# A DeltaNet solve with 16x16 blocks on VectorE, joined to 32x32 on TensorE

## The chip, the cores and the metric

The kernel runs on one core of a Trainium2 chip. The metric is the device time of one execution in microseconds (us); lower is better. Below, TensorE is PE (its weight loads PEld), VectorE DVE, ScalarE ACT, GpSimd POOL and SyncE SP.

## What is computed

A two-layer decoder trunk over 256 tokens of width 2048, float32: layer 0 mixes with mLSTM and retention heads, layer 1 with a gated DeltaNet, each followed by a SwiGLU FFN. The change lies in the DeltaNet of layer 1. It has 32 value heads and works in chunks; for each head it solves a unit lower triangular system with the strictly lower matrix `a`:

```python
k_beta = k * beta[..., None]
a = jnp.where(strict, jnp.einsum('bhnld,bhnsd->bhnls', k_beta, k) * decay, 0.0)
rhs = jnp.concatenate([v * beta[..., None], k_beta * jnp.exp(g_cum)[..., None]], axis=-1)
sol = lax.linalg.triangular_solve(a, rhs, left_side=True, lower=True, unit_diagonal=True)
```

The kernel computes the inverse T of (I + a) explicitly, in chunks of 128 tokens: first the inverses of small diagonal blocks, then larger ones from pairs. With blocks T1 above, T2 below and A21 between, the lower left block of the joined inverse is -T2 A21 T1.

## The kernel before

All big matrix products stream their weights in *units*: 512 KB of weights (two tiles of 128 rows by 512 columns) are loaded by SP into one of four buffers `wraw`; ACT rounds them to `whi` (L957), DVE makes the remainder `wlo` (L1386), and PE multiplies: eight products with `whi` (L527, L528), then four with `wlo` (L533). A unit's buffers are free again when PE has finished it, so ACT and DVE may run at most four units ahead; PE waits for `whi` at the start of a unit and for `wlo` before the four low products. The input projection of layer 1 has 192 units.

The DeltaNet itself is woven into these units in four *rounds* of 8 heads x 2 chunks (16 systems each), which start at units 20, 57, 94 and 131 and have 43 *slots*. After each unit every engine calls `gdn(r, s)` with the slot's number. PE does slot s behind unit start + s; ACT and DVE do it behind their piece of unit start + s + 2 (`AHEAD`), so slot s of DVE stands two units ahead of PE's in the order of the weights. Each engine runs its own instructions strictly in this order. Below, "unit n" is the nth after a round's start and Pn is the start of its four low products.

What a round does around the change:

- slots 7 and 8: DVE builds the systems `A_` (L1764); slot 9: DVE convolves V0 (L1747, 12 instructions), ACT gathers the 32x32 diagonal blocks into `diag` (L1243); POOL clears `TT` and `T`.
- slot 10: DVE turns the diagonal blocks within quarters of 32 partitions (`leaf_start`: a transpose of 1024 elements a partition, L1771, and a copy of 512, L1773). Each partition then works on one system's block: 16 systems, the even columns in one half of a quarter's 32 partitions and the odd ones in the other.
- slots 10 to 20: `leaf` does 31 elimination steps, three a slot; each is a product (L1782) and a subtraction (L1785) with a drain behind each. The inverse's transposes `leaf_T` and `leaf_TT` are made in slot 20 (`leaf_end`, L1789 and L1792).
- slot 13: PE turns V0 (L732), and ACT copies it (L1210); slot 15: PE turns Q (L580), and ACT takes its taps from PSUM (L1181), each behind its `whi`.
- slot 21: ACT copies `leaf_TT` into `TT` (L1259), POOL copies `leaf_T` into `T` (L496); DVE convolves Q.
- slots 23, 24: PE joins 32x32 inverses to 64x64, first `level_q` (L772), then, after a copy by ACT, `level_t` (L780, L782); slots 27, 28: 64x64 to 128x128 (L765).
- In the last round DVE has, besides, products of gates with outputs (L1889) at units 146 and 149, which are slots 13 and 16.

Of the kernel before, what the change touches and what calls it, by code (L numbers as in the profile page):

```python
# [25 lines left out]
ALU = mybir.AluOpType  # L26
# [33 lines left out]

HALF = P // 2
CONST_PARTS = [("ident", 128), ("upto", 128), ("after", 128), ("ones", 128), ("neg", 384),
               ("low_up", 256), ("decay", RH * 256), ("freq", 128),
               ("leaf_eye", LEAF * LEAF // 2)]
CONST_AT = {}
# [7 lines left out]
def shape_constants():  # L73
# [4 lines left out]
    def put(name, v):  # L78
        lo, hi = CONST_AT[name]
        c[:, lo:hi] = v  # L80
# [7 lines left out]
    put("low_up", np.concatenate([a > b, a <= b], 1))  # L88
    i, half = np.arange(LEAF)[None, :, None], np.arange(LEAF // 2)[None, None, :]
    parity = (np.arange(P) % LEAF // (LEAF // 2))[:, None, None]  # L90
    put("leaf_eye", (i == 2 * half + parity).reshape(P, -1))
    t = np.arange(SEQ)[None, :]
# [65 lines left out]
ROOT_AT = counts("k", "q")  # L158
LEAF_AT = counts("T", "TT")
LEVEL_PSUM = counts("q32_0", "q32_1", "T32_0", "T32_1", "q64_0", "q64_1", "TT64_0", "TT64_1")  # L160
LEVEL_COPY = counts("q32_0", "q32_1", "q64_0", "q64_1")
# [6 lines left out]
def build(nc, A, out):  # L168

    with ExitStack() as ctx:  # L170
# [86 lines left out]
        leaf_p = at(83 * KB, [P, 256])  # L257
        lead = at(84 * KB, [P, LEAF, LEAF])
        leaf_t = at(88 * KB, [P, LEAF, LEAF // 2])
        diag = at(90 * KB, [P, M * HV, LEAF])  # L260
        leaf_T = at(84 * KB, [P, M * HV, LEAF])
        leaf_TT = at(86 * KB, [P, M * HV, LEAF])
        Q32 = at(88 * KB, [P, M, HV, LEAF])
# [65 lines left out]
        et_set = sem("et_set")  # L329
        diag_set = sem("diag_set")  # L330
        leaf_set = sem("leaf_set")
        tt_zero = sem("tt_zero")
# [140 lines left out]
        def _(pool):  # L473
# [14 lines left out]
            def gdn(r):  # L488
                pool.wait_ge(a_set, D_AT(r, 1))
                nc.gpsimd.memset(TT[:], 0.0).then_inc(tt_zero, 1)  # L490
                pool.wait_ge(eat_psum, D_AT(r, 1))
                nc.gpsimd.memset(T[:], 0.0)
# [29 lines left out]
        def _(pe):  # L522
# [198 lines left out]
            def gdn(r, s):  # L721
# [40 lines left out]
                def quarters(to, left, right):  # L762
# [3 lines left out]
                    mm.then_inc(lev_psum, 1)  # L766

                def level_q(c, to):

                    for h in range(HV):  # L770
                        for b in (0, 2):
                            mm = nc.tensor.matmul(to[quarter(b), h * LEAF:(h + 1) * LEAF], A_[quarter(b + 1), c, h, quarter(b)],  # L772
                                                  TT[quarter(b + 1), c, h, quarter(b + 1)], start=True, stop=True)
                    mm.then_inc(lev_psum, 1)
# [48 lines left out]
                if s == 15:  # L823
                    pe.wait_ge(tok_copy, TOK_AT(r, V0))
                    conv_transposes(Q, aux[0])
                halves = [aux[1][:, c * NB:(c + 1) * NB] for c in range(M)]
                if s == 23:
                    pe.wait_ge(et_copy, D_AT(r, 1))
                    pe.wait_ge(tt_in, r + 1)
                    level_q(0, halves[0])  # L830
                    level_q(1, halves[1])
# [113 lines left out]
        def _(act):  # L945
# [229 lines left out]
            def gdn(r, s):  # L1175
# [77 lines left out]
                if s == 15:  # L1253
                    tap(Q)
                if s == 21:
                    act.wait_ge(leaf_set, LEAF_AT(r, "TT"))
# [115 lines left out]
        def _(dve):  # L1372
# [361 lines left out]
            def gdn(r, s):  # L1734
# [26 lines left out]
                def system(c):  # L1761
# [4 lines left out]
                    a.then_inc(a_set, 1)  # L1766

                def leaf_start():

                    dve.wait_ge(diag_set, r + 1)  # L1770
                    V.transpose(lead[:].rearrange("p j i -> p (j i)"),  # L1771
                                diag[:].rearrange("p k j -> p j k").unsqueeze(2).to_broadcast([P, LEAF, 2, LEAF // 2]))
                    V.tensor_copy(leaf_t[:].rearrange("p i c -> p (i c)"), C["leaf_eye"])  # L1773
                    dve.drain()

                def leaf(first, last):

                    for j in range(first, last):
                        rows, cols = LEAF - 1 - j, j // 2 + 1
                        p = leaf_p[:, 0:rows * cols].rearrange("p (i c) -> p i c", c=cols)  # L1780
                        below = leaf_t[:, j + 1:, 0:cols]
                        V.tensor_tensor(p, lead[:, j, j + 1:].unsqueeze(2).to_broadcast([P, rows, cols]),  # L1782
                                        leaf_t[:, j:j + 1, 0:cols].to_broadcast([P, rows, cols]), ALU.mult)
                        dve.drain()  # L1784
# [3 lines left out]
                def leaf_end():  # L1788
                    V.transpose(leaf_T[:].rearrange("p k (c e) -> p c e k", e=2), leaf_t[:].rearrange("p i c -> p c i")  # L1789
                                ).then_inc(leaf_set, 1)  # L1790
                    dve.drain()
                    V.transpose(leaf_TT[:].rearrange("p k i -> p (k i)"), leaf_T[:].rearrange("p k j -> p (k j)")).then_inc(leaf_set, 1)  # L1792

# [29 lines left out]
                if s == 10:  # L1823
                    leaf_start()
                if 10 <= s <= 20:
                    leaf(max(0, 3 * (s - 10) - 1), 3 * (s - 10) + 2 if s < 20 else LEAF - 1)
                if s == 20:
                    leaf_end()
                if s == 21:
# [131 lines left out]
```

## Time and profile before

| | |
|---|---|
| time, median of 3 runs | 2863.43 us (2860.95 to 2864.47) |
| profiled execution: its time, its span | 2861.21 us, 2859.4 us |
| PE busy | 2788.6 us (98%), 13652 instructions |
| PEld busy | 2298.6 us (80%) |
| DVE busy | 1569.4 us (55%), 1942 instructions |
| ACT busy | 1368.2 us (48%) |
| POOL busy | 74.2 us (3%) |
| PE on the chain that ended last | 86% of the span, DVE 7%, ACT 4% |
| mean granted clock of TensorE | 0.996 |

The span runs from the first to the last instruction of one profiled execution, and the 1.8 us around it belong to its time. A PE counted as busy need not be at its peak, since the ends of products are modelled and overlap. "Granted clock" is the share of full speed that the chip gave TensorE. Idle time of an engine that is not the bottleneck costs nothing.

### The profile page before, as it was taken

The page shows a single profiled execution, that of the slowest core. Times are in us where ns is not written, and L with a number is a line of the kernel's source. Part 1 is how long each engine was busy: PE and PEld are TensorE (multiplying, and loading weights), DVE is VectorE, ACT ScalarE, POOL GpSimd, SP SyncE. Part 2 cuts the span into 40 slices and gives each one's busy share as a digit, 9 for nine tenths or more (in the row PEclk, how much of TensorE's full clock was granted, in tenths as well). Part 3 has the DMA queues.
Part 4 walks back from the last instruction along what each step waited for, and adds up shares of the span by engine and source line. Part 5 has one row for each costly group of instructions (what it writes and reads, how often), then busy time and mean ns, then how long its engine had stood idle before and what let it go on. Part 6 is the DMA issues. An engine that isn't in the chain of part 4 may idle for free.

```text
span 2859.4 us, 37257 instructions
## 1 busy us (share of the span) xinstructions
PE 2788.6 (98%) x13652; PEld 2298.6 (80%) x13652; DVE 1569.4 (55%) x1942; ACT 1368.2 (48%) x1874; POOL 74.2 (3%) x55
## 2 busy tenths in 40 slices
PE   8999999999999999998999999999999999999998
PEld 6788788888888888886878787887888888888886
DVE  4554565545445445458586768665554454454444
ACT  5354455444444444455665656554454444444443
POOL 0000000000000000000000010000000000000000
PEclk9999999999999999999999999999999999999999
DMA  7464466666666666654454545555666666666664
GB/s 235 147 199 151 136 191 185 192 190 187 190 187 191 187 189 191 181 167 135 123 157 126 153 128 156 162 169 185 189 185 194 188 190 189 187 191 189 206 191 141
DMA packets 261266, 502.63 MB, mean 176 GB/s; under 512 B 20112, under 2 KB 20368, under 8 KB 260624
## 3 DMA queue, kind: packets, MB, share of 16 engines
q1 hardware_dynamic: 259504, 494.60, 58.0%
q0 software_dynamic: 816, 3.15, 0.3%
q10 hardware_dynamic: 816, 3.15, 0.3%
q8 instruction: 82, 1.34, 0.2%
q14 instruction: 48, 0.39, 0.0%
HBM read 495.59 MB, written 5.24 MB: 175 GB/s over the span
## 4 chain that ended last, share of the span: by engine, by line
PE 86%; DVE 7%; ACT 4%; issue 1%; DVEq 1%; ACTq 0%; DMA 0%; SPq 0%
PE acc L533 27%; PE acc L527 26%; PE acc L528 26%; DVE wlo L1386 2%; PE aux L759 2%; PE aux L580 2%; DVE arena L1785 1%; ACT whi L957 1%; DVE arena L1782 1%; DVE arena L1747 1%; PE aux L765 1%; DVE const L1747 1%; ACT arena L1302 0%; DVEq L1784 0%; DVEq L1751 0%
## 5 line engine op out<-in xcount | busy, mean ns | idle before, releaser
L1386 DVE TENSOR_TENSOR wlo<-wraw,whi 128x1024 fp32r<-128x1024 f32 x928 | 1151.4, 1247 | 1111.4 <-ACT whi L957 1102.9
L957 ACT ACTIVATE whi<-wraw 128x1024 fp32r<-128x1024 f32 x928 | 974.1, 1060 | 1096.0 <-PE acc L533 1043.9
L527 PE MATMUL acc<-whi,hT_hi 128*128 128x512 f32 x2624 | 1039.8, 396 | 7.5 <-ACT whi L957 7.1
L528 PE MATMUL acc<-whi,hT_lo 128*128 128x512 f32 x2624 | 1024.3, 390 | 0.0
L533 PE MATMUL acc<-wlo,hT_hi 128*128 128x512 f32 x2624 | 708.0, 392 | 27.9 <-DVE wlo L1386 27.2
L533 PEld LDWEIGHTS acc<-wlo,hT_hi 128*128 128x128 f32 x2624 | 489.7, 188 | 146.3 <-DVE wlo L1386 45.8
L527 PEld LDWEIGHTS acc<-whi,hT_hi 128*128 128x128 f32 x2624 | 493.9, 188 | 109.8 <-issue 7.9
L528 PEld LDWEIGHTS acc<-whi,hT_lo 128*128 128x128 f32 x2624 | 494.1, 188 | 100.8 <-issue 1.0
L527 PE MATMUL acc<-whi,arena 128*128 128x512 f32 x1088 | 428.4, 394 | 3.2 <-ACT whi L957 3.2
L528 PE MATMUL acc<-whi,arena 128*128 128x512 f32 x1088 | 425.8, 391 | 0.0
L533 PE MATMUL acc<-wlo,arena 128*128 128x512 f32 x1088 | 293.4, 391 | 0.0
L527 PEld LDWEIGHTS acc<-whi,arena 128*128 128x128 f32 x1088 | 204.9, 188 | 46.9 <-ACT whi L957 3.4
L533 PEld LDWEIGHTS acc<-wlo,arena 128*128 128x128 f32 x1088 | 204.3, 188 | 45.4
L528 PEld LDWEIGHTS acc<-whi,arena 128*128 128x128 f32 x1088 | 205.0, 188 | 44.5
L973 ACT ACTIVATE arena<-acc,rstd 128x512 f32<-128x512 f32 x120 | 75.4, 682 | 4.9 <-DVE arena L1889 3.6
L479 POOL COPY x<-xs 128x1024 f32 x16 | 19.2, 1198 | 2214.5 <-DVE xs L1424 2214.5
L1405 DVE SCALAR_TENSOR_TENSOR hT_lo<-aux,gains,hT_hi 128x256 fp32r<-128x256 f32 x56 | 23.2, 477 | 35.6 <-ACT hT_hi L992 35.6
L1747 DVE SCALAR_TENSOR_TENSOR const<-aux,arena,const 128x255 f32<-128x255 f32 (+2 forms) x96 | 39.6, 475 | 1.2
L1747 DVE SCALAR_TENSOR_TENSOR arena<-aux,arena,arena 128x255 f32<-128x255 f32 (+2 forms) x96 | 39.5, 473 | 1.2
L759 PEld LDWEIGHTS aux<-arena,arena 128*128 128x128 f32 x320 | 38.2, 192 | 1.2
L759 PE MATMUL aux<-arena,arena 128*128 128x128 f32 x320 | 38.3, 275 | 0.0
L1785 DVE TENSOR_TENSOR arena<-arena,arena 128x126 f32<-128x126 f32 (+22 forms) x124 | 31.9, 257 | 10.0 <-issue 0.9
(239 smaller groups left out, 1172.9 us busy)
## 6 DMA issues: line engine op xcount, KB each, us to landing
wraw<-in_l_w_in SPq DMA_DIRECT2D x304, 512.0 KB, 3.8
wraw<-in_l_w_gate SPq DMA_DIRECT2D x176, 512.0 KB, 3.7
wraw<-in_l_w_up SPq DMA_DIRECT2D x176, 512.0 KB, 3.7
wraw<-in_l_w_down SPq DMA_DIRECT2D x176, 512.0 KB, 4.1
wraw<-in_l_w_out SPq DMA_DIRECT2D x96, 512.0 KB, 4.6
o_rounds<-arena POOLq DMA_DIRECT2D x3, 1024.0 KB, 4.8
arena<-o_rounds ACTq DMA_DIRECT2D x3, 1024.0 KB, 6.2
x<-in_x SPq DMA_DIRECT2D x4, 512.0 KB, 6.0
```

Source lines behind the costliest of these rows:

```text
L527: nc.tensor.matmul(pair[m], hi[:, k, tok], wh, start=first, stop=False)
L528: nc.tensor.matmul(pair[m], lo[:, k, tok], wh, start=False, stop=False)
L533: mm = nc.tensor.matmul(pair[m], hi[:, k, m * P:(m + 1) * P], wl, start=False, stop=k_last)
L580: mm = nc.tensor.transpose(dst[:, t * SEQ + m * P:t * SEQ + (m + 1) * P], src(m, t), ident)
L759: mm = nc.tensor.matmul(to[:, head(h)], left(h), right(h), start=True, stop=True)
L765: mm = nc.tensor.matmul(to[0:HALF, h * HALF:(h + 1) * HALF], left(h), right(h), start=True, stop=True)
L957: nc.scalar.activation(whi[:, s, :], wraw[:, s, :], ACT.Copy).then_inc(hi_done, 1)
L973: a = nc.scalar.activation(dst(m), acc[parity][:, m, :], func, scale=rstd[:, m:m + 1])
L1386: V.tensor_tensor(wlo[:, s, :], wraw[:, s, :], whi[:, s, :].bitcast(F32), ALU.subtract).then_inc(lo_done, 1)
L1747: a = V.scalar_tensor_tensor(dst[:, t, lag:], aux[0][:, t * SEQ:(t + 1) * SEQ - lag], conv_w[:, w, CW - 1 - lag:CW - lag], dst[:, t, lag:] ...
L1782: V.tensor_tensor(p, lead[:, j, j + 1:].unsqueeze(2).to_broadcast([P, rows, cols]), leaf_t[:, j:j + 1, 0:cols].to_broadcast([P, rows, cols ...
L1785: V.tensor_tensor(below, below, p, ALU.subtract)
```

## The change

DVE now inverts 16x16 diagonal blocks: 15 elimination steps in slots 10 to 17, two a slot (one in slot 10). `leaf_start` transposes half as many elements and then picks, by two masks `half`, the right diagonal block for each half of a quarter's partitions (a scalar product and a scalar_tensor_tensor). `leaf_end` moves to slot 17 and spreads the result into a 32x32 block diagonal (two scalar products into `spread`) before the two transposes. POOL cuts the lower left 16x16 `corner` out of each 32x32 diagonal block. PE then joins: in slot 18 `join_q` makes Q = corner-block times inverse (4 blocks x 16 systems = 64 products of 32x32 by 32x32), ACT copies it to `Q16`, in slot 19 `join_t` makes the correction and its transpose (128 products); in slot 20 DVE subtracts both from `leaf_T` and `leaf_TT`, which then go on as before. The waits: PE's `join_q` waits for the solve (`solved`), ACT's copy for `join_q`, `join_t` for the copy, DVE's subtraction for `join_t`.

```diff
+SOLVE = LEAF // 2
 CONST_PARTS = [("ident", 128), ("upto", 128), ("after", 128), ("ones", 128), ("neg", 384),
                ("low_up", 256), ("decay", RH * 256), ("freq", 128),
-               ("leaf_eye", LEAF * LEAF // 2)]
+               ("solve_eye", SOLVE * SOLVE), ("half", 2), ("corner", LEAF)]
...
-    i, half = np.arange(LEAF)[None, :, None], np.arange(LEAF // 2)[None, None, :]
-    parity = (np.arange(P) % LEAF // (LEAF // 2))[:, None, None]
-    put("leaf_eye", (i == 2 * half + parity).reshape(P, -1))
+    put("solve_eye", np.eye(SOLVE).reshape(1, -1))
+    upper = a % LEAF < SOLVE
+    put("half", np.concatenate([upper, ~upper], 1))
+    put("corner", ~upper & (np.arange(LEAF)[None, :] < SOLVE))
...
-        lead = at(84 * KB, [P, LEAF, LEAF])
-        leaf_t = at(88 * KB, [P, LEAF, LEAF // 2])
+        lead = at(84 * KB, [P, SOLVE, LEAF])
+        solve_a, solve_t = (at((86 + n) * KB, [P, SOLVE, SOLVE]) for n in range(2))
+        corner = at(88 * KB, [P, M * HV, LEAF])
         diag = at(90 * KB, [P, M * HV, LEAF])
-        leaf_T = at(84 * KB, [P, M * HV, LEAF])
-        leaf_TT = at(86 * KB, [P, M * HV, LEAF])
+        spread = at(84 * KB, [P, LEAF, SOLVE])
+        leaf_T = at(86 * KB, [P, M * HV, LEAF])
+        leaf_TT = at(90 * KB, [P, M * HV, LEAF])
+        Q16 = at(84 * KB, [P, M * HV, LEAF])
...
+                pool.wait_ge(diag_set, r + 1)
+                nc.gpsimd.tensor_tensor(corner[:], diag[:], C["corner"].unsqueeze(1).to_broadcast([P, M * HV, LEAF]), ALU.mult
+                                        ).then_inc(corner_set, 1)
...
+
+                def join_q(to):
+
+                    for n in range(M * HV):
+                        for b in range(4):
+                            mm = nc.tensor.matmul(to[quarter(b), n * LEAF:(n + 1) * LEAF], corner[quarter(b), n, :], leaf_TT[quarter(b), n, :],
+                                                  start=True, stop=True)
+                    mm.then_inc(join_psum, 1)
+
+                def join_t(to, to_t):
+
+                    for n in range(M * HV):
+                        for b in range(4):
+                            nc.tensor.matmul(to[quarter(b), n * LEAF:(n + 1) * LEAF], Q16[quarter(b), n, :], leaf_T[quarter(b), n, :],
+                                             start=True, stop=True)
+                        for b in range(4):
+                            mm = nc.tensor.matmul(to_t[quarter(b), n * LEAF:(n + 1) * LEAF], leaf_T[quarter(b), n, :], Q16[quarter(b), n, :],
+                                                  start=True, stop=True)
+                    mm.then_inc(join_psum, 1)
...
+                if s == 18:
+                    pe.wait_ge(et_copy, D_AT(r, 1))
+                    pe.wait_ge(corner_set, r + 1)
+                    pe.wait_ge(solved, r + 1)
+                    join_q(halves[0])
+                if s == 19:
+                    pe.wait_ge(join_copy, r + 1)
+                    join_t(halves[1], halves[0])
                 if s == 23:
-                    pe.wait_ge(et_copy, D_AT(r, 1))
...
+                if s == 18:
+                    act.wait_ge(join_psum, JOIN_PSUM(r, "q16"))
+                    nc.scalar.activation(Q16[:].rearrange("p k n -> p (k n)"), aux[1][:, 0:NB], ACT.Copy).then_inc(join_copy, 1)
...
+                half = lambda e: C["half"][:, e:e + 1]
+
                 def leaf_start():

                     dve.wait_ge(diag_set, r + 1)
-                    V.transpose(lead[:].rearrange("p j i -> p (j i)"),
-                                diag[:].rearrange("p k j -> p j k").unsqueeze(2).to_broadcast([P, LEAF, 2, LEAF // 2]))
-                    V.tensor_copy(leaf_t[:].rearrange("p i c -> p (i c)"), C["leaf_eye"])
+                    V.transpose(lead[:].rearrange("p j i -> p (j i)"), diag[:].rearrange("p k (e j) -> p j e k", e=2))
+                    V.tensor_copy(solve_t[:].rearrange("p i c -> p (i c)"), C["solve_eye"])
+                    dve.drain()
+                    V.tensor_scalar(solve_a[:], lead[:, :, 0:SOLVE], half(0), None, ALU.mult)
+                    dve.drain()
+                    V.scalar_tensor_tensor(solve_a[:], lead[:, :, SOLVE:], half(1), solve_a[:], op0=ALU.mult, op1=ALU.add)
                     dve.drain()

                 def leaf(first, last):

                     for j in range(first, last):
-                        rows, cols = LEAF - 1 - j, j // 2 + 1
+                        rows, cols = SOLVE - 1 - j, j + 1
                         p = leaf_p[:, 0:rows * cols].rearrange("p (i c) -> p i c", c=cols)
-                        below = leaf_t[:, j + 1:, 0:cols]
-                        V.tensor_tensor(p, lead[:, j, j + 1:].unsqueeze(2).to_broadcast([P, rows, cols]),
-                                        leaf_t[:, j:j + 1, 0:cols].to_broadcast([P, rows, cols]), ALU.mult)
+                        below = solve_t[:, j + 1:, 0:cols]
+                        V.tensor_tensor(p, solve_a[:, j, j + 1:].unsqueeze(2).to_broadcast([P, rows, cols]),
+                                        solve_t[:, j:j + 1, 0:cols].to_broadcast([P, rows, cols]), ALU.mult)
                         dve.drain()
                         V.tensor_tensor(below, below, p, ALU.subtract)
                         dve.drain()

                 def leaf_end():
-                    V.transpose(leaf_T[:].rearrange("p k (c e) -> p c e k", e=2), leaf_t[:].rearrange("p i c -> p c i")
-                                ).then_inc(leaf_set, 1)
-                    dve.drain()
-                    V.transpose(leaf_TT[:].rearrange("p k i -> p (k i)"), leaf_T[:].rearrange("p k j -> p (k j)")).then_inc(leaf_set, 1)
+
+                    for e in range(2):
+                        V.tensor_scalar(spread[:, e * SOLVE:(e + 1) * SOLVE, :], solve_t[:], half(e), None, ALU.mult)
+                    dve.drain()
+                    V.transpose(leaf_T[:].rearrange("p k (e c) -> p c e k", e=2), spread[:].rearrange("p i c -> p c i"))
+                    dve.drain()
+                    dve.wait_ge(corner_set, r + 1)
+                    V.transpose(leaf_TT[:].rearrange("p k i -> p (k i)"), leaf_T[:].rearrange("p k j -> p (k j)")).then_inc(solved, 1)
+                    dve.drain()
+
+                def leaf_join():
+
+                    dve.wait_ge(join_psum, JOIN_PSUM(r, "T16"))
+                    for to, n in ((leaf_T, 1), (leaf_TT, 0)):
+                        V.tensor_tensor(to[:], to[:], aux[1][:, n * NB:(n + 1) * NB].rearrange("p (k n) -> p k n", n=LEAF), ALU.subtract
+                                        ).then_inc(leaf_set, 1)
...
-                if 10 <= s <= 20:
-                    leaf(max(0, 3 * (s - 10) - 1), 3 * (s - 10) + 2 if s < 20 else LEAF - 1)
+                if 10 <= s <= 17:
+                    leaf(max(0, 2 * (s - 10) - 1), 2 * (s - 10) + 1)
+                if s == 17:
+                    leaf_end()
                 if s == 20:
-                    leaf_end()
+                    leaf_join()
```

## Rows read from the trace of the kernel before

**Rows 1.** Chain of waits of core 0, 1308 to 1356 us: shares by line.
```profile
by line: DVE wlo L1386 27.8%; DVE arena L1785 13.6%; DVE arena L1782 9.1%; issue 8.8%; DVE arena L1747 8.8%; PE acc L533 5.0%; DVE arena L1771 4.2%; ACT arena L1210 4.1%; DVEq L1751 4.1%; DVEq L1784 4.0%; DVE arena L1789 2.4%; ACT whi L957 
```

**Rows 2.** Timeline of PE, rounds 1 and 3: start us, us, engine, line, operation.
```profile
1458.23 1.20 PE L533 MATMUL acc<-wlo,hT_hi 128*128 128x512 f32 x4 [0.56 <-DVE wlo L1386]
...
1477.49 1.07 PE L533 MATMUL acc<-wlo,hT_hi 128*128 128x512 f32 x4
1480.21 1.07 PE L533 MATMUL acc<-wlo,hT_hi 128*128 128x512 f32 x4
...
1502.63 1.20 PE L533 MATMUL acc<-wlo,hT_hi 128*128 128x512 f32 x4 [1.38 <-DVE wlo L1386]
...
1755.02 1.21 PE L533 MATMUL acc<-wlo,hT_hi 128*128 128x512 f32 x4 [0.55 <-DVE wlo L1386]
...
1801.84 1.19 PE L533 MATMUL acc<-wlo,hT_hi 128*128 128x512 f32 x4 [1.35 <-DVE wlo L1386]
```

**Rows 3.** Timeline of PE, round 0: low products of five units.
```profile
1310.06 1.20 PE L533 MATMUL acc<-wlo,hT_hi 128*128 128x512 f32 x4 [0.54 <-DVE wlo L1386]
...
1314.86 1.20 PE L533 MATMUL acc<-wlo,hT_hi 128*128 128x512 f32 x4 [1.77 <-DVE wlo L1386]
...
1321.42 1.21 PE L533 MATMUL acc<-wlo,hT_hi 128*128 128x512 f32 x4
...
1325.18 1.07 PE L533 MATMUL acc<-wlo,hT_hi 128*128 128x512 f32 x4
...
1354.95 1.20 PE L533 MATMUL acc<-wlo,hT_hi 128*128 128x512 f32 x4 [1.31 <-DVE wlo L1386]
```

**Rows 4.** Timeline of DVE, round 0, slots 9, 10 and 20.
```profile
1303.78 5.09 DVE L1747 SCALAR_TENSOR_TENSOR const<-aux,arena,const 128x255 f32<-128x255 f32 x12
1308.78 1.22 DVE L1386 TENSOR_TENSOR wlo<-wraw,whi 128x1024 fp32r<-128x1024 f32 x1
1309.92 2.10 DVE L1771 STREAM_TRANSPOSE arena<-arena 128x1024 f32<-128x1024 f32 x1
1311.93 0.40 DVE L1773 COPY arena<-const 128x512 f32<-128x512 f32 x1
1312.40 0.19 DVE L1782 TENSOR_TENSOR arena<-arena,arena 128x31 f32<-128x31 f32 x1
...
1313.58 1.23 DVE L1386 TENSOR_TENSOR wlo<-wraw,whi 128x1024 fp32r<-128x1024 f32 x1
...
1345.68 1.16 DVE L1789 STREAM_TRANSPOSE arena<-arena 128x512 f32<-128x512 f32 x1 [0.43 <-issue]
1346.94 0.71 DVE L1792 STREAM_TRANSPOSE arena<-arena 128x512 f32<-128x512 f32 x1
```

**Rows 5.** Lines of DVE by form: busy us, mean ns of one | idle before.
```profile
L1889 DVE TENSOR_TENSOR arena<-arena,arena 128x1024 f32<-128x1024 f32 x8 | 9.8, 1219 | 0.1
...
L1558 DVE TENSOR_SCALAR arena<-const,gate_t 128x128 f32<-128x128 f32 x4 | 1.1, 281 | 0.0
```

**Rows 6.** Timeline of ACT, round 0: taps of Q and what follows.
```profile
1323.54 1.57 ACT L1181 ACTIVATE arena<-aux,arena 128x256 f32<-128x256 f32 x4 [2.50 <-PE aux L580]
1324.98 2.02 ACT L957 ACTIVATE whi<-wraw 128x1024 fp32r<-128x1024 f32 x2
```

**Rows 7.** Timelines of PE and PEld, round 0: small products of slots 23, 24.
```profile
1350.38 1.20 PE L772 MATMUL aux<-arena,arena 32*32 32x32 f32 x64 [0.37 <-ACT arena L1259]
...
1356.96 0.11 PEld L780 LDWEIGHTS aux<-arena,arena 32*32 32x32 f32 x2 [0.17 <-issue]
...
1358.10 0.19 PEld L527 LDWEIGHTS acc<-whi,hT_hi 128*128 128x128 f32 x1
...
1360.04 1.07 PE L533 MATMUL acc<-wlo,hT_hi 128*128 128x512 f32 x4
```

**Rows 8.** Windows in round 1: us, PE busy (x), PEclk granted, DMA share, GB/s.
```profile
1460.90:1464.31 3.41, 1.63 (x9) 1.00 0.21 55
1464.31:1467.72 3.41, 3.41 (x14) 0.50 0.62 159
```

More of the change, by code:

```diff
@@ L159 @@
 LEAF_AT = counts("T", "TT")
+JOIN_PSUM = counts("q16", "T16")
 LEVEL_PSUM = counts("q32_0", "q32_1", "T32_0", "T32_1", "q64_0", "q64_1", "TT64_0", "TT64_1")
@@ L330, in build @@
         diag_set = sem("diag_set")
+        corner_set = sem("corner_set")
+        solved = sem("solved")
+        join_psum = sem("join_psum")
+        join_copy = sem("join_copy")
         leaf_set = sem("leaf_set")
```

## The prediction

> **What bounds the kernel now.** Over the whole program TensorE is on the chain that ended last for 86% of the span (table above); the question is where it is not. Of the four rounds of the DeltaNet layer I read the chain of waits for the stretch from slot 10 to slot 24 of the first round: there VectorE is the chain, with `wlo` 27.8%, L1785 13.6% and L1782 9.1% [rows 1]. So here TensorE waits for VectorE, and what VectorE no longer does can be worth its time.
>
> How much, the starts of the low products (L533) show. An undisturbed unit takes 2.72 us (1477.49 to 1480.21) [rows 2]: 1.81 of high products, then 0.91 of low ones. P12 and P24 are the low products of the 12th and the 24th unit after a round's first. In round 0 they start at 1310.06 and 1354.95, 44.89 us apart [rows 3]; in round 1 44.40 and in round 3 46.82 [rows 2]; round 2 repeats round 1 with 44.57. TensorE's own work in between is 12 x 2.72 = 32.6, two groups of eight transposes (0.9 each: P16 is 3.76 after P15 [rows 3], which is 2.72, 0.9 and some start-up) and one block of small products (about 1.4, below): 35.8. The rest, 9.1 + 8.6 + 8.8 + 11.0 = 37.5 us in four rounds, is waiting for VectorE. Its cause is in VectorE's timeline [rows 4]: the convolution of V0 (5.09) and the two transposes and copies of slot 10 use up the lead of four buffers, and then every unit has 1.14 of `wlo` and six solve instructions (3.0 to 3.4 a unit against 2.72), before 1.16 + 0.71 of end transposes and another convolution.
>
> **The change, part by part.** I walk through round 0. P12 stays at 1310.06, since slots before 10 are untouched.
>
> Slot 10 on VectorE. Now the first transpose starts at 1309.92, the copy 2.01 later, the first step at 1312.40, and the next `wlo` starts at 1313.58, so two steps cost 1.18 [rows 4]. Afterwards the transpose moves half as much (1.0; the bound above is the 1.16 of L1789), the copy half as much (0.33 to the next start), then a scalar product of 256 elements (128 take 281 ns [rows 5], 255 of the convolution 5.09/12 = 0.42 each [rows 4]: 0.42, with the drain 0.49), a scalar_tensor_tensor of 256 (0.48, with the drain 0.55) and one step (0.6). The next `wlo` starts at 1312.95 instead of 1313.58: 0.63 gained, and P13 moves from 1314.86 to 1314.23. TensorE still waits there for about 1.4.
>
> Slots 11 to 17. Two steps a slot, of 28 to 64 elements, 1.17 to 1.26 (the same 1.18 for 31 and 30 elements), with `wlo` 2.3 to 2.4 a unit, under TensorE's 2.72. No stall of the low products is left. Counting from 1312.95, unit 18's `wlo` could start at 1324.8; but ScalarE cannot give `whi` of unit 18 before its taps of Q, which wait for the transposes after P15. Before, these taps started 2.12 after P15 and `whi` 1.44 later [rows 3, 6]. P15 stays 6.56 behind P13, as before, and goes to 1320.8, so `whi` of unit 18 ends at 1325.4, unit 19's `wlo` starts at 1327.75, slot 17 at 1328.9, its two steps end at 1329.95.
>
> leaf_end in slot 17. Two scalar products of 256 into `spread` (0.33 + 0.42, drain 0.07), the scattering transpose (1.16) and the plain one (0.71) [rows 4], drains 0.1: the solve is ready at 1332.8. POOL's corner product needs only `diag` and is long done.
>
> **The wait that is added.** join_q comes behind unit 18 in TensorE's queue. P16 = P15 + 2.72 + 0.9 = 1324.4, P18 = 1329.85, its end 1330.8. So TensorE waits for about 2.0 us (bounds: 1.3, if scalar products ran at the speed of the copy and the scattering transpose at the plain one's 0.71; 2.6, with every new VectorE price at its upper row). Behind it stand all of unit 19's products; VectorE and ScalarE are two units ahead and lose nothing that the buffers do not cover.
>
> **The price of the small products.** Every such product stands twice in the trace. Today 32 products on two tiles of the array stand as x64 and take 1.20 with the last one's tail; 48 products on three tiles (L780, L782) run from 1356.96 to 1358.10, 1.14 [rows 7]. Both have 16 products per tile: the time goes by products per tile, 64 ns each plus 0.12, and the tiles overlap. Around a block some 0.25 more goes (P25 comes 5.09 after P24: 2.72 + 0.9 + 1.02 leave 0.45 [rows 3, 7]); I take 0.35 in all. join_q has four tiles x 16 products: 1.02 + 0.35. join_t has the same four tiles x 32: 2.05 + 0.35. Together 3.8 a round. From above: no more than two tiles at once gives 192 x 32 ns = 6.1 + 0.7; the issue rate seen (96 records in 1.02) gives 4.1 + 0.7 = 4.8; no overlap at all 192 x 64 ns = 12.3 + 0.7. I take four at once, since two and three both overlap fully.
>
> The rest hides. The Q16 copy (0.7; two `whi` of twice the size take 2.02 [rows 6]) runs while TensorE does unit 19 (2.7), and `whi` of unit 21 follows some 6 us before it is due. leaf_join (two subtractions, 1.4) ends 1.4 after join_t, the TT copies 2.5 later, three units before level_q; the 0.4 wait of L772 for L1259 [rows 7] goes. The convolution of Q now falls into free time. Without that cover it would cost what it costs today, some 2 us of waits at P24.
>
> **The sum.** join_q starts at 1332.85, unit 19's high products at 1334.0, join_t at 1336.9, unit 20's high products at 1339.1, P20 at 1341.0, P23 at 1349.2, level_q at 1350.2, P24 at 1353.3 instead of 1354.95. From P12 to P24 43.2 us: saved 1.7, 1.2 and 1.35 in rounds 0 to 2. In round 3 two gate products (1.22 each [rows 5]) sit in slots 13 and 16 and push the solve out by about 2.1: 45.3 against 46.8, saved 1.5. Sum 5.7. Against it stands the clock: in round 1 a stall of 1.8 in slot 10 was followed by a stretch of 3.41 us at a granted 0.50 [rows 8], that is at 1.2 instead of 2.4 GHz, worth 1.7; in the other three rounds the same stall had no such stretch. Today that loss is swallowed by the later waits for VectorE; after the change TensorE is the bound behind join_q, and a stretch at half clock there costs in full. One in four of 4 x 1.7: minus 1.7. I forecast 4 us less than the profiled execution's 2861.2 us, so 2857.2; the median of the runs is 2.2 above that execution: 2859.4 us.
>
> The Trainium skill ("TensorEngine Tiling (Array Packing)", Gotcha 1: PSUM Pressure) says that different row tiles cannot access the same PSUM bank simultaneously, and join_q's four row tiles all write one bank. In this trace L772 does so with two row tiles and L780 with L782 with three tiles in no more time [rows 7], so the trace disagrees so far. By the page's rule nothing would overlap and the sum would be 2896 us, as in the third rival; by the rows it is the one above.
>
> **Rivals.**
> 1. The join wait vanishes: VectorE's pieces in slots 10 and 17 are cheaper than I put them and the taps of Q come earlier. Then 4 x 2.0 more is gained: 2851 us. For it: a copy of 512 elements takes only 0.40 [rows 4], so one-source instructions can be quick. Against: the 128-element scalar product does not show that speed [rows 5].
> 2. The clock falls in every round behind the join wait: 4 x 1.7 instead of one: no gain, 2864 to 2865 us.
> 3. Slower: only two tiles at once, or fewer. The products cost 3.1 more a round at two at once: -4 + 12.3, 2872 us, about 8 slower. It decides once the products cost 1.0 a round more than my 3.8: then the 4 us are gone. With no overlap, +9.2 a round: 2896 us. For it: four row tiles at once are nowhere in the trace.
> 4. The products issue no faster than 96 in 1.02 us: +1.0 a round, 2863.5 us, no difference.
>
> **How the numbers follow.** Forecast 0.50 (its own range 2855 to 2863); rival 1 0.13; rival 2 0.10; rival 3 0.15 (0.05 of it with no overlap); rival 4 0.12. A change of 0.2%, 5.7 us, is about what this kernel's measurement can tell from none. Of the forecast's 0.50, 0.18 lie beyond 5.7 faster; with rival 1 faster is 0.31. Slower: rival 3 and 0.03 of rivals 2 and 4: 0.18. The same: 0.51. The range 2851 to 2872 leaves out no overlap at all and the outer part of rival 1.
>
> **What would show it.** In the profile of the changed kernel: P12 to P24 of about 43.2 in rounds 0 to 2; no L533 wait for VectorE between P14 and P24; a TensorE wait for the end transpose ahead of join_q of about 2.0; the join blocks at 1.1 and 2.2 us, with 128 and 256 records. Wrong it would be by a join_t over 3 us, by a wait at join_q under 1 or over 3, or by half-clock stretches in more than one round.

## The result

The changed kernel takes 2889.9 us (median of 4 runs, 2889.6 to 2892.5); the kernel before took 2863.95 beside it (4 runs, 2861.0 to 2864.6). The ratio is 1.0096 [1.0084, 1.0109]: 26 us slower. The forecast was 2859.4, with a range of 2851 to 2872; the result lies above the range and on the other side.

The page of the profiled execution after (own time 2889.6 us, mean granted clock 0.992), busy time first, then the costliest lines that read the working area, then the instruction queue. L540, L541 and L546 are now the two high products and the low product that stood at L527, L528 and L533:

```profile
span 2887.8 us, 40121 instructions
...
PE 2820.1 (98%) x15188; PEld 2319.0 (80%) x15188; DVE 1538.9 (53%) x1838; ACT 1370.7 (47%) x1878; POOL 78.6 (3%) x59
...
q8 instruction: 94, 1.54, 0.2%
...
PE 90%; ACT 4%; DVE 4%; issue 1%; DVEq 1%; ACTq 0%; DMA 0%; SPq 0%
...
L540 PE MATMUL acc<-whi,arena 128*128 128x512 f32 x1088 | 430.8, 396 | 3.2 <-ACT whi L996 3.2
L541 PE MATMUL acc<-whi,arena 128*128 128x512 f32 x1088 | 429.3, 395 | 0.0
L546 PE MATMUL acc<-wlo,arena 128*128 128x512 f32 x1088 | 298.2, 395 | 0.0
```

VectorE has 30 us less of work (1569.4 before), and TensorE's share of the chain rose from 86% to 90%. The span grew by 28.4 us. Three sums account for it, from the starts of the low products:

| part | before | after | difference |
|---|---|---|---|
| P12 to P24, rounds 0 to 3 | 44.9, 44.4, 44.6, 46.8 | 45.6, 47.0, 48.8, 51.8 | +12.4 |
| the four stages whose units read `arena` | 91.4, 245.2, 185.0, 242.6 | 93.1, 249.9, 188.5, 247.2 | +14.5 |
| all the rest | | | +1.5 |

The second line is in stages that the diff does not touch. They are the output projections and the down projections of both layers, 272 units in all. Timelines of PE in the last down projection, of the kernel before and of the one after:

```profile
2701.74 1.08 PE L533 MATMUL acc<-wlo,arena 128*128 128x512 f32 x4
2704.49 1.08 PE L533 MATMUL acc<-wlo,arena 128*128 128x512 f32 x4
2707.23 1.08 PE L533 MATMUL acc<-wlo,arena 128*128 128x512 f32 x4
```

```profile
2702.09 1.09 PE L546 MATMUL acc<-wlo,arena 128*128 128x512 f32 x4
2704.89 1.09 PE L546 MATMUL acc<-wlo,arena 128*128 128x512 f32 x4
2707.70 1.09 PE L546 MATMUL acc<-wlo,arena 128*128 128x512 f32 x4
```

A unit takes 2.80 us instead of 2.75, at full clock and with no wait. Units that read hT_hi and hT_lo take 2.72 in both kernels. So it is the operand in the working area that got slower to read. The change shrank the constants ahead of that area (2816 to 2594 floats a partition), and the area now starts 896 bytes earlier in each partition: its start leaves 192 when divided by 1024, where it left 64.

The first line is the join. VectorE after, from the last solve steps of round 0 to the subtraction:

```profile
1315.81 1.22 DVE L1428 TENSOR_TENSOR wlo<-wraw,whi 128x1024 fp32r<-128x1024 f32 x1
1316.94 1.13 DVE L1815 STREAM_TRANSPOSE arena<-arena 128x512 f32<-128x512 f32 x1
1317.96 0.28 DVE L1816 COPY arena<-const 128x256 f32<-128x256 f32 x1
1318.32 0.35 DVE L1818 TENSOR_SCALAR arena<-arena,const 128x256 f32<-128x256 f32 x1
1318.75 0.48 DVE L1820 SCALAR_TENSOR_TENSOR arena<-arena,const,arena 128x256 f32<-128x256 f32 x1
...
1319.89 1.22 DVE L1428 TENSOR_TENSOR wlo<-wraw,whi 128x1024 fp32r<-128x1024 f32 x1
...
1336.66 0.62 DVE L1838 TENSOR_SCALAR arena<-arena,const 128x256 f32<-128x256 f32 x2
1337.36 1.08 DVE L1840 STREAM_TRANSPOSE arena<-arena 128x512 f32<-128x512 f32 x1
1338.51 0.71 DVE L1843 STREAM_TRANSPOSE arena<-arena 128x512 f32<-128x512 f32 x1
...
1348.59 1.28 DVE L1850 TENSOR_TENSOR arena<-arena,aux 128x512 f32<-128x512 f32 x2 [3.96 <-PE aux L796]
```

PE after, in the same stretch:

```profile
1317.08 1.20 PE L546 MATMUL acc<-wlo,hT_hi 128*128 128x512 f32 x4 [0.58 <-DVE wlo L1428]
...
1321.17 1.20 PE L546 MATMUL acc<-wlo,hT_hi 128*128 128x512 f32 x4 [1.06 <-DVE wlo L1428]
...
1336.70 1.07 PE L546 MATMUL acc<-wlo,hT_hi 128*128 128x512 f32 x4
1339.37 1.28 PE L785 MATMUL aux<-arena,arena 32*32 32x32 f32 x128 [1.60 <-DVE arena L1843]
...
1342.53 1.08 PE L546 MATMUL acc<-wlo,hT_hi 128*128 128x512 f32 x4
1343.53 0.26 PE L793 MATMUL aux<-arena,arena 32*32 32x32 f32 x8
...
1344.91 0.23 PE L793 MATMUL aux<-arena,arena 32*32 32x32 f32 x4
1347.58 0.21 PE L793 MATMUL aux<-arena,arena 32*32 32x32 f32 x1 [2.44 <-issue]
```

The two views answer to [rows 2 to 4]. The new `wlo` of slot 10 comes 4.08 after unit 12's, where it was 4.80. After P13 no low product waits for VectorE until `join_q`. It waits 1.60 for the end transpose and then goes through its 128 records in 1.1 us. `join_t` is another matter: 1.4 us into it, TensorE stops: 2.6 us pass from one start to the next (2.44 of them idle), and the row names no engine, only "issue". From first to last record `join_t` takes 4.8, 5.0, 3.9 and 5.2 us in the four rounds. Each has a gap, of 2.6, 2.3, 1.7 and 3.1 us from start to start, behind 166, 151, 136 and 249 of its 256 records. The weight-load side of TensorE says the same for L793 (its 2.0 at L785 is the wait for the solve ahead of `join_q`); the first waits of PEld from 1335 to 1365 us:

```profile
engine line waited for: us in total, times, longest us
PEld aux L793 <- issue: 2.9, 2, 2.6
PEld aux L785 <- issue: 2.0, 1, 2.0
```

What can starve an engine that waits for no other? The DMA view of the kernel after has a kind of packet that carries instructions. In 1340 to 1350 us it shows:

```profile
q8 instruction: 3, 0.05, 2.0%
```

and in 1344.8 to 1347.6 us, which is the gap:

```profile
q8 instruction: 1, 0.02, 2.9%
```

The packets are of 16 KB, and over the program there are 94 of them, where there were 82. PE and PEld each gained 1536 instructions (13652 to 15188), together 3072, which is 256 for each new packet. `join_q` is thus worth one packet of instructions and `join_t` two, run at 1.1 us a packet. In a stretch of 12 us around the gap of round 1 there were four packets after, which start at 1489.5, 1493.6, 1497.2 and 1500.7 us, and one before (1489 to 1501 us, after, then before):

```profile
q8 instruction: 4, 0.07, 2.3%
```

```profile
q8 instruction: 1, 0.02, 0.5%
```

So the suspicion from the trace: when they are wanted fastest, packets start some 3.5 to 4.2 us apart (4.2 and 3.8 in round 0; 4.1, 3.6 and 3.5 in round 1), and `join_t` eats two in 2.1.

### The profile page after: what moved, and what is told of

It reads as the page before. It is cut to its first block, busy times and chain, and to the rows that moved or that the text cites. A ratio compares the mean times of both kernels' runs of the same rounds, so it can differ in the third digit from the quotient of the medians.

```text
span 2887.8 us, 40121 instructions
## 1 busy us (share of the span) xinstructions
PE 2820.1 (98%) x15188; PEld 2319.0 (80%) x15188; DVE 1538.9 (53%) x1838; ACT 1370.7 (47%) x1878; POOL 78.6 (3%) x59
## 4 chain that ended last, share of the span: by engine, by line
PE 90%; ACT 4%; DVE 4%; issue 1%; DVEq 1%; ACTq 0%; DMA 0%; SPq 0%
PE acc L540 28%; PE acc L546 27%; PE acc L541 27%; PE aux L593 2%; PE aux L772 2%; DVE wlo L1428 1%; ACT whi L996 1%; PE aux L778 1%; DVE const L1789 1%; ACT arena L1344 0%; PE aux L745 0%; PE aux L766 0%; PE aux L752 0%; ACT arena L1220 0%; DVE arena L1806 0%
## 5 line engine op out<-in xcount | busy, mean ns | idle before, releaser
L540 PE MATMUL acc<-whi,hT_hi 128*128 128x512 f32 x2624 | 1044.2, 398 | 7.4 <-ACT whi L996 7.0
L541 PE MATMUL acc<-whi,hT_lo 128*128 128x512 f32 x2624 | 1028.1, 392 | 0.0
L546 PE MATMUL acc<-wlo,hT_hi 128*128 128x512 f32 x2624 | 705.9, 391 | 10.3 <-DVE wlo L1428 9.5
L546 PEld LDWEIGHTS acc<-wlo,hT_hi 128*128 128x128 f32 x2624 | 493.6, 189 | 118.7 <-DVE wlo L1428 13.9
L540 PEld LDWEIGHTS acc<-whi,hT_hi 128*128 128x128 f32 x2624 | 496.0, 189 | 110.5 <-issue 7.8
L541 PEld LDWEIGHTS acc<-whi,hT_lo 128*128 128x128 f32 x2624 | 496.0, 189 | 101.1 <-issue 1.0
L540 PE MATMUL acc<-whi,arena 128*128 128x512 f32 x1088 | 430.8, 396 | 3.2 <-ACT whi L996 3.2
L541 PE MATMUL acc<-whi,arena 128*128 128x512 f32 x1088 | 429.3, 395 | 0.0
L546 PE MATMUL acc<-wlo,arena 128*128 128x512 f32 x1088 | 298.2, 395 | 0.0
L540 PEld LDWEIGHTS acc<-whi,arena 128*128 128x128 f32 x1088 | 203.9, 187 | 53.4 <-ACT whi L996 3.4
L546 PEld LDWEIGHTS acc<-wlo,arena 128*128 128x128 f32 x1088 | 204.2, 188 | 50.5
L541 PEld LDWEIGHTS acc<-whi,arena 128*128 128x128 f32 x1088 | 203.9, 187 | 49.4
L593 PEld LDWEIGHTS aux<-const,xs 128*128 128x128 f32 x272 | 31.7, 140 | 4.5
```

The source lines that it names most:

```text
L540: nc.tensor.matmul(pair[m], hi[:, k, tok], wh, start=first, stop=False)
L541: nc.tensor.matmul(pair[m], lo[:, k, tok], wh, start=False, stop=False)
L546: mm = nc.tensor.matmul(pair[m], hi[:, k, m * P:(m + 1) * P], wl, start=False, stop=k_last)
L593: mm = nc.tensor.transpose(dst[:, t * SEQ + m * P:t * SEQ + (m + 1) * P], src(m, t), ident)
```

## The experiments

Two theories were set apart first. PLACE: the 14.5 us come from the address of the working area alone. SUPPLY: the gap in `join_t` is a lack of instructions and goes when the burst is cut. The rivals were that the joins themselves, or their buffers, slow the later stages, and that the small products are slow for a reason of the array or of PSUM.

**a_place**: the change, with the area at the same place as before.

```diff
-        arena0 = (nc.sbuf_base + 63) // 64 * 64
+        arena0 = (nc.sbuf_base + 63) // 64 * 64 + 896
```

> The changed kernel with its working area moved up by 896 bytes, so that it starts where it starts in the kernel before (the smaller constants had moved it down by 896). Theory PLACE: the units that read their stationary operand from that area (272 of the 928, output and down projections) take 2.80 us after and 2.75 before only because of where it starts. Then these units return to 2.75 and the kernel gains 272 x 0.053 = 14.5 us: about 2875.5 us. Rival: something else in the change slows them (clock, transfers): no change, 2890.

Measured 2876.6 us against 2863.1 (ratio 1.0052 [1.0035, 1.0069]), 13.3 less than the changed kernel. The four stages went back to 91.4, 245.2, 185.7 and 242.6 us; P12 to P24 stayed long (193.7 in sum). PLACE holds.

**b_shift128**: the kernel before, area moved so that its start leaves 192 when divided by 1024, as in the changed kernel.

```diff
-        arena0 = (nc.sbuf_base + 63) // 64 * 64
+        arena0 = (nc.sbuf_base + 63) // 64 * 64 + 128
```

> The kernel before with its working area moved up by 128 bytes and nothing else, so that its start modulo 1024 is 192, as in the changed kernel (64 before). PLACE, if only the start modulo 1024 counts: the 272 units go from 2.75 to 2.80, 14.5 us slower, about 2878. If the start modulo 128 is what counts: no change, 2864.

Measured 2875.3 us, 12.3 over the kernel before (ratio 1.0046 [1.0029, 1.0063]). The units read 2.80 and the rounds were unchanged at 180.7. One constant of the allocator, with no instruction added, costs half of what the change cost.

**b_align**: the kernel before, area at a multiple of 1024.

```diff
-        arena0 = (nc.sbuf_base + 63) // 64 * 64
+        arena0 = (nc.sbuf_base + 63) // 64 * 64 + 960
```

> The kernel before with its working area moved up by 960 bytes, to a multiple of 1024. PLACE: the 272 units fall to the 2.72 us of the units that read from the other area: 272 x 0.027 = 7.3 us faster, about 2856.5. Rival: 2.75 is the price of that area for another reason: 2864.

A miss: 2873.3 us (ratio 1.0042 [1.0025, 1.0059]), with units of 2.79. The idea that a round address is the fast one fell. What was left was a dependence on the address without a rule.

**b_shift64**: the same with + 64, which leaves 128.

> The kernel before with its working area moved up by 64 bytes, so that its start modulo 1024 is 128, which is that of the area whose units take 2.72. Theory PLACE by the start modulo 1024 (0 gave 2.79, 64 gives 2.75, 192 gives 2.80): 2.72, 7.3 us faster, 2856. Rival: something coarser than 1024 counts (the distance to the streamed weights): anything between 2.72 and 2.80.

Measured 2855.9 us against 2863.6 (ratio 0.9976 [0.9966, 0.9986]): faster than the kernel before. The last down projection of b_shift64 on PE:

```profile
2700.27 1.07 PE L533 MATMUL acc<-wlo,arena 128*128 128x512 f32 x4
2702.99 1.07 PE L533 MATMUL acc<-wlo,arena 128*128 128x512 f32 x4
2705.71 1.07 PE L533 MATMUL acc<-wlo,arena 128*128 128x512 f32 x4
```

2.72 a unit, the rate of the units that don't read the area. By the start's remainder to 1024: 0 gives 2.79, 64 gives 2.75, 128 gives 2.72, 192 gives 2.80. These are four points of one kernel, not a law, and remainders to 256 or 512 would be the same four. One remainder was seen at two addresses: the areas of b_shift128 and of the changed kernel start 1024 bytes apart, and both give 2.80.

**a_split**: a_place with `join_t` cut in two bursts of 64 products, one behind unit 19 and one behind unit 20.

```diff
+                def join_tt(to_t):
...
                 if s == 19:
                     pe.wait_ge(join_copy, r + 1)
-                    join_t(halves[1], halves[0])
+                    join_t(halves[1])
+                if s == 20:
+                    join_tt(halves[0])
```

> a_place with the 128 products of join_t in two halves: 64 behind unit 19 and 64 behind unit 20. Theory SUPPLY: the gaps of 1.8 to 3.1 us inside join_t, which no other engine ends, come from TensorE running out of fetched instructions in a burst of 512 (256 loads, 256 products) straight behind another of 256. With a unit between the halves the gaps vanish, and most stretches at half clock behind them too: four rounds x 2.4 us and some 4 us of clock, less 4 x 0.35 for one more block: 11 to 13 us under a_place, 2863. Rival CLOCK or ARRAY: the gap belongs to the products themselves (four tiles, one bank): the halves take as long together as the whole, no gain or 1 us slower than a_place.

Measured 2863.1 us, 13.5 less than a_place and level with the kernel before (ratio 1.0001 [0.9991, 1.0011]). Round 0 of a_split on PE:

```profile
1333.36 1.28 PE L785 MATMUL aux<-arena,arena 32*32 32x32 f32 x128 [1.60 <-DVE arena L1849]
1336.51 1.07 PE L546 MATMUL acc<-wlo,hT_hi 128*128 128x512 f32 x4
1337.51 1.29 PE L793 MATMUL aux<-arena,arena 32*32 32x32 f32 x128
1340.67 1.07 PE L546 MATMUL acc<-wlo,hT_hi 128*128 128x512 f32 x4
```

The same products, on the same operands, tiles and PSUM banks, run in 1.3 us a burst with their tail. P12 to P24 is 43.3, 43.7, 46.0 and 47.9. In rounds 2 and 3 the clock fell to half in the join (from 1630.5 and from 1780.7 us, 3.4 us each), and gaps of 0.5 to 0.8 were left. Bursts come every 4.17 us here, about as often as packets come; in this run the closest start 3.3 to 3.6 us apart. The run also gives a price for the half clock. P18 to P19 took 7.4 in round 2, which had a stretch of 3.4 us at half clock there, and 5.8 in rounds 0 and 1, which had none: 1.6 us.

**b_burst**: the kernel before, with nothing of the change but two idle bursts, 64 products behind unit 18 and 128 behind unit 19, on inputs that are ready; their results are not used.

```diff
+                def burst(to, times):
+
+                    for n in range(M * HV):
+                        for b in list(range(4)) * times:
+                            a = A_[quarter(b), n // HV, n % HV, quarter(b)]
+                            mm = nc.tensor.matmul(to[quarter(b), n * LEAF:(n + 1) * LEAF], a, a, start=True, stop=True)
...
+                if s == 18:
...
+                    burst(halves[0], 1)
+                if s == 19:
+                    burst(halves[1], 2)
```

> The kernel before, with nothing changed but 64 idle products on four tiles behind unit 18 and 128 behind unit 19 of each round (their results are overwritten). Theory SUPPLY: a gap of 1.8 to 3.1 us inside the second burst, in all four rounds, though no new wait, copy or operand is there. Rival: the gap comes of join_t's operands or of its wait for the copy: bursts of 1.1 and 2.1 us without a gap.

One run: 2876.9 us. The gap is there without any join, in all four rounds, 2.4, 2.9, 2.2 and 3.2 us, and there are smaller ones of 0.6 in round 1 and 1.8 in round 3. Second burst of b_burst on PE, its end in round 0 and the whole of it in round 3:

```profile
1340.79 0.98 PE L774 MATMUL aux<-arena 32*32 32x32 f32 x90 [2.25 <-issue]
...
1793.51 1.22 PE L774 MATMUL aux<-arena 32*32 32x32 f32 x120
1796.32 1.29 PE L774 MATMUL aux<-arena 32*32 32x32 f32 x128 [1.59 <-issue]
1800.62 0.33 PE L774 MATMUL aux<-arena 32*32 32x32 f32 x8 [3.01 <-issue]
```

The two gaps of round 3 lie 128 records apart, and these 128 have as many weight loads: 256 instructions, one packet. The same holds between kernels. Counted in TensorE's records from P12, the gaps of one round stand at the same place of a packet whatever the kernel: at 14, 127, 112 and 97 beyond a multiple of 128 in rounds 0 to 3 (in the burst kernels one less in rounds 1 to 3). All 28 gaps over 0.12 us inside the small products of the changed kernel, a_place, a_split, b_burst, b_burst2, a_later and a_best stand there. TensorE stops where one packet's worth of instructions ends, not at a certain product of the join.

**b_burst2**: the same number of products on two tiles only, so that each burst runs at half the rate.

```diff
-                        for b in list(range(4)) * times:
+                        for b in (0, 1) * 2 * times:
```

> b_burst with the same number of idle products (64, then 128 a round) on two tiles of the array instead of four, so that they can issue only half as fast (32 ns a product, 2.05 and 4.1 us). SUPPLY: what starves is a rate of issue, so the same number of instructions at half the rate has a smaller gap: less than 1 us in the second burst, and no more than b_burst in time. Rival: the gap is a fixed price of so many instructions: again about 2.4 us on top of 4.1.

One run: 2879.2 us. The gaps shrank to 1.0, 1.6, 0.5 and 1.4 (and 1.2 beside it in round 3), as a supply with a fixed rate asks, though only one round came under the 1 us that was expected. The whole was 2.3 us longer than b_burst, where no more had been expected: the slower products cost somewhat more than the smaller gap gave back. Both sizes missed; the direction held, and the rival's 2.4 is not there.

**a_nojoin**: a_place with one of the 16 systems joined (the line changes in `join_q` and in `join_t`); it leaves out the joins of the other 15.

```diff
-                    for n in range(M * HV):
+                    for n in range(1):
```

> a_place with 1 of 16 systems joined: 12 small products a round instead of 192, all waits kept (the joins of 15 systems are left out). It shows what the smaller solve alone is worth. By the prediction's sum P12 to P24 is 43.2 less 3.1 us of products, about 40 in each of rounds 0 to 2, against 44.4 to 44.9 before; and no gap that no engine ends. If the gap were not the supply of instructions but the joining itself, it would still be there.

One run: 2847.7 us. P12 to P24 is 39.9, 40.2, 40.2 and 44.4, 164.7 in sum against 180.7 before, and no gap is left. This is what moving the solve to 16x16 gives TensorE when the joins are nearly free: 16 us. The waits of `join_q` for VectorE are still in these times, 1.6 in rounds 0 to 2 and 3.3 in round 3, where a stretch of 6.8 us at half clock begins in the wait.

**a_later**: a_split with the whole join one slot later, in slots 19, 20 and 21, so that the solve is ready.

```diff
-                if s == 18:
+                if s == 19:
                     pe.wait_ge(et_copy, D_AT(r, 1))
...
-                if s == 19:
+                if s == 20:
...
-                if s == 20:
+                if s == 21:
                     leaf_join()
```

> a_split with everything of the join one slot later: join_q behind unit 19, the two halves of join_t behind units 20 and 21, ScalarE's copy and VectorE's subtraction moved likewise. Theory WAIT: join_q waits for VectorE's end transposes because it comes one unit too early (1.6 us in rounds 0 to 2, about 4 in round 3, with stretches at half clock behind the waits of rounds 2 and 3). One unit is 2.7 us, so the wait goes in three rounds and most of it in the fourth: 4 x 1.6 + 2 + about 4 of clock: 10 to 13 us under a_split, 2851. Rival: the engines' later waits (ScalarE's TT copies now end just before level_q) give it back: no gain, 2863.

Measured 2855.7 us against 2863.6 (ratio 0.9975 [0.9966, 0.9985]), 7.4 less than a_split where 10 to 13 were expected. The wait at `join_q` is gone in rounds 0 to 2, 0.7 of it is left in round 3, and round 0 takes 41.6. But one burst of round 1 and one of round 2 still starve. Round 1 of a_later:

```profile
1492.78 0.21 PE L800 MATMUL aux<-arena,arena 32*32 32x32 f32 x1 [1.76 <-issue]
1495.66 1.87 PE L546 MATMUL acc<-wlo,hT_hi 128*128 128x512 f32 x4
```

The low product behind it takes 1.87 instead of 1.07: half the clock follows the gap. This gap stands behind 127 of the burst's 128 records, that of round 2 (1.9 from start to start) behind 124. Here the place of the packet's end matters. In the two cut `join_t` bursts of a_split, a_later and a_best, where it fell at the burst's record 38 or earlier, none of 11 starved; where it fell between records 97 and 127, 9 of 13 did. The later join moved these ends by one unit's 12 records. Three bursts in three slots are at the edge of the supply; whether the wait that is gone had also given it time was not tried by itself.

**a_best**: a_later with the area where it leaves 128.

```diff
-        arena0 = (nc.sbuf_base + 63) // 64 * 64
+        arena0 = (nc.sbuf_base + 63) // 64 * 64 + 960
```

> a_later with its working area 64 bytes higher, so that it starts at 128 modulo 1024. PLACE: the 272 units go from 2.75 to 2.72 as they did in b_shift64, 7.3 us: 2848.4, which is also 7.5 us under b_shift64, what the change is worth with its products apart and both kernels at the good place. Rival: the gains of place and join do not add (the rounds' arrays lie in the same area): 2851 to 2855.

Measured 2850.6 us (5 runs, 2845.9 to 2853.1) against 2862.8 (ratio 0.9951 [0.9938, 0.9965]), the fastest of those that compute the whole: 12 us under the kernel before. It lies between the forecast (2848.4) and the rival's 2851 to 2855, and the interval, some 4 us to either side, holds the forecast and most of the rival's range, so that it does not tell whether the gains add in full. The working-area units took 2.72. b_shift64 had 7.8 of the 12 by the place alone. The other 4.5 are a difference between two sets of runs, with intervals of 4 and 3 us to either side, and not clear of them; at the old place, a_later against the kernel before, the 16x16 blocks with the burst cut and the join later bring 7.9.

## Why the prediction was wrong, step by step

**VectorE's walk** was right. The slot-10 pieces were forecast to bring `wlo` 0.63 earlier (4.17 after unit 12's) and brought 0.72 (4.08) in round 0; in rounds 1 and 2 P13 still came 4.4 after P12. Slots 11 to 17 left no stall of the low products. The spread and transposes were forecast at 2.8 with drains and took 2.6 (1336.66 to 1339.22).

**The wait at join_q** was forecast at 2.0 (1.3 to 2.6) and was 1.6 in rounds 0 to 2. In round 3, where the two gate products push the solve out, the step put it 2.1 longer, at 4.1, and the row shows 3.4.

**Four tiles overlap**, as the step had it. The Trainium skill ("TensorEngine Tiling (Array Packing)", Gotcha 1: PSUM Pressure) says that row tiles cannot access one PSUM bank at once; `join_q`'s four write one bank, each its own 32 partitions, and 128 records start within 1.09 us, 8.5 ns apart. This case does not show that rule. It also settles rival 4, an issue rate of no more than 96 records in 1.02 us. Rival 3, by which the kernel was to be slower, had the right sign for the wrong reason.

**The price of join_t failed**: "join_t has the same four tiles x 32: 2.05 + 0.35". The term was built from rows of blocks with 96 and 128 records [rows 7] and doubled. The doubling assumed that TensorE's instructions are always there, a term put at nothing without a row for it; none of the four rivals has it either. From P19 to P20 5.2 us was forecast; 7.9, 9.0, 9.0 and 9.6 were measured, 14.6 more in all. The gaps are 9.7 of it; round 0, with no half clock, is explained by its gap alone (5.2 + 2.6), and the remaining 4.9 fall in the three rounds where the clock fell behind the gap. b_burst made the same gap with no join, a_split took it away in rounds 0 and 1 (and left 0.8 at most) with the same products, and the gaps stand one packet apart, so that the mechanism is shown. The stretch from P19 to P20 is 14.6 of the 18.2 by which the four rounds exceed the forecast's 174.9; the rest is mainly one unit of round 2 at half clock (4.49 instead of 2.72) and the stretch from P18 to P19 in round 3 (9.9, of which the walk had some 8.1). With the burst cut, round 0 gave 43.3 where the walk had said 43.2; all four gave 180.9, 6 over the forecast, nearly all of it in rounds 2 and 3, where the clock fell and small gaps were left.

The Trainium skill ("Runtime: NRT & Kernel Launch", Instruction fetch mechanics) says that instructions come in blocks of 16 KiB with 256 instructions each, that PE holds 2048, and that fetching hides behind issue. The block size agrees with the trace (94 packets for 82, 3072 instructions more). That it hides does not: round 0 of the changed kernel stalled some 610 instructions of TensorE after `join_q` began (256 of `join_q`, 24 of unit 19, and the 166 product records of `join_t` ahead of the gap with their weight loads, 332).

**The clock.** The forecast put one half-clock stretch, which was to cost 1.7 us, in four rounds. After, there were four in the join stretches of rounds 1 to 3 (two of 3.4 us, two of 6.8), which was one of the signs named for a wrong forecast. Round 3, windows of the kernel after with PE busy and, behind POOL's, the granted clock:

```profile
1793.16:1799.99 6.83, 5.64 (x137) 4.83 (x138) 4.28 (x5) 2.49 (x3) 0.00 (x0) 0.50 0.38 116
1799.99:1806.81 6.82, 3.93 (x263) 3.29 (x262) 0.71 (x2) 1.06 (x1) 0.00 (x0) 1.00 0.48 156
1806.81:1810.20 3.39, 3.39 (x9) 2.64 (x8) 3.39 (x7) 2.46 (x4) 2.63 (x3) 0.50 0.09 12
```

`join_q`'s wait stands before and in the first window, whose clock is 0.50 (1.2 GHz), `join_t`'s gap in the second, and behind it the clock is 0.50 again. How much the clock cost is an estimate. Beyond the forecast and the gap, rounds 1 and 2 took 1.5 and 3.8 us more, beside stretches of 3.4 and 6.8 us at half clock, and a_split's stretch of 3.4 cost 1.6: about half a stretch's length. So the price of one stretch was right, their number was not. Rival 2 had the clock fall behind the wait at `join_q`. In the changed kernel that happened in round 3 alone, in a_split in rounds 2 and 3.

**"The rest hides" was right, and "The sum" left out a term.** `level_q` waited for nothing in any round, as the step on the rest had it. But the sum ran from P12 to P24 and put every other stage at nothing. It counted the instructions of the change and not where its smaller constants move everything behind them. That place cost 14.5 us in the profiled execution; a_place and b_shift128 show it from both sides (13.3 and 12.3 us in the medians). No range built from the rounds alone could hold it. Without it, and with the burst as it is, the time was 2876.6; with the area back and the burst cut, 2863.1, 3.7 over the forecast.

Left open: why the address of the stationary operand matters (the records of the weight loads themselves last 187 to 189 ns at every place), why four of the 13 bursts with a late packet end did not starve, and what decides whether the clock falls behind a wait. Joins with fewer instructions, or products of the join spread through a unit instead of standing in a block, were not tried.

## What to carry to other kernels

Small products cost TensorE instructions as well as array time. Here packets of 256 instructions started 3.3 us apart at the closest and mostly 3.5 to 4.2, and 64 small float products used one up in 1.1. 128 such products one unit behind another 64 starved in every round. Blocks of 64 every 4.2 us starved in some rounds, so cuts further apart are the next thing to try; no run here has them. And when an edit changes the size of anything allocated ahead of an operand, note its start address before and after: the same kernel ran 2.72 to 2.80 us a unit by the address alone, and by that some 19 us over the program (b_shift64 against b_shift128), more than the 16 us that the 16x16 solve could give; the place is worth a search of its own.

## What had not been expected of the hardware

- A 128x512 product of the units (four bytes an element) is slower by up to 3% by the place of the stationary operand: 2.72, 2.75, 2.79 and 2.80 us a unit where the start of its area leaves 128, 64, 0 and 192 when divided by 1024.
- A burst of 512 TensorE instructions, one unit behind a burst of 256, starves by 1.7 to 3.1 us, and the wait has no releaser in the profile. The signs are "issue" inside a block, a 16 KB instruction packet beside it, and gaps that stand a multiple of 256 instructions apart.
- In one execution of a_best the granted clock read 0.95 in stretches of up to 1130 us, and the units took 2.72 us there all the same (317 of the 380 in the longest stretch within 0.02).
- Records of small products on four tiles start 8.5 ns apart; at half clock 13 (128 in 1.69 us, round 3).
